# The activation of 32 clamped-SwiGLU experts: Silu on ScalarE, a clamp on the product, and three VectorE steps in place of five

## What is computed

```python
logits = xt @ w_router + b_router                # top 4 of 32, softmax over the four
gu = xblk @ w_gu[e] + b_gu[e]                    # 1024 -> 2048, gate half | linear half
x_glu = jnp.minimum(gu[:, :F], 7.0)
x_lin = jnp.clip(gu[:, F:], -7.0, 7.0)
act = x_glu * jax.nn.sigmoid(1.702 * x_glu) * (x_lin + 1.0)
return act @ w_down[e] + b_down[e]               # weighted by the gate and summed per token
```

## Time and profile before

| | us |
|---|---|
| median of 3 runs | 1244.47 |
| lowest, highest run | 1243.40, 1245.21 |
| span of the profiled execution | 1242.5 |

### The profile page before, as it was taken

The page is one execution under the profiler, slowest core; times in us unless marked ns, Lnnn a source line. Parts: engine busy times, 40 slices in busy tenths (PEclk is TensorE's granted clock), DMA queues, the critical chain, the costliest instruction groups (busy, mean ns, idle before and its releaser), DMA issues.

```text
span 1242.5 us, 40004 instructions
## 1 busy us (share of the span) xinstructions
PE 1147.6 (92%) x17556; PEld 886.8 (71%) x17557; DVE 1148.4 (92%) x870; ACT 933.7 (75%) x823; POOL 503.6 (41%) x69
## 2 busy tenths in 40 slices
PE   5999999999999999999999999999999999999984
PEld 3454556977777777777777777777777777888751
DVE  5855577989999999999999999999999999999987
ACT  4334444878888888888888888888888888888852
POOL 0110400027777776667766666631010011266620
PEclk9999999999999999999999999999999999999998
DMA  9605854999999999999999999999999999999986
GB/s 349 221 9 203 297 189 160 337 349 404 420 417 415 419 416 416 418 416 416 415 418 416 418 412 420 420 416 409 419 413 419 411 410 415 421 415 418 413 330 248
DMA packets 73255, 458.08 MB, mean 369 GB/s; under 512 B 10076, under 2 KB 10588, under 8 KB 23632
## 3 DMA queue, kind: packets, MB, share of 16 engines
q1 hardware_dynamic: 68480, 445.30, 88.5%
q0 software_dynamic: 3472, 8.21, 1.7%
q10 hardware_dynamic: 1152, 2.19, 0.6%
HBM read 443.26 MB, written 24.77 MB: 377 GB/s over the span
## 4 chain that ended last, share of the span: by engine, by line
PE 45%; DVE 32%; issue 19%; ACT 3%; DMA 1%; DVEq 0%; SPq 0%; ACTq 0%
DVE ring L416 22%; PE ps L437 16%; PE ps L473 11%; PE ps L1130 8%; PE ps L430 3%; PE ps L1233 3%; ACT ring L413 1%; DVE arena L503 1%; DVE arena L506 1%; DVE arena L518 1%; DVE arena L509 1%; DVE arena L512 1%; DMA ring<-in_w_in_dram 1%; PE ps L1170 1%; PE ps L458 1%
## 5 line engine op out<-in xcount | busy, mean ns | idle before, releaser
L495 POOL DMA_INDIRECT planes<-arena,slot_row x31 | 480.5, 15502 | 568.4 <-ACT arena L525 568.4
L416 DVE SCALAR_TENSOR_TENSOR ring<-ring 128x2048 f16<-128x2048 f32 x290 | 660.0, 2333 | 5.9 <-ACT ring L413 5.3
L413 ACT ACTIVATE ring<-ring 128x2048 f16<-128x2048 f32 x290 | 544.0, 1905 | 47.3 <-DMA ring<-in_w_gu_dram 25.4
L437 PE MATMUL ps<-arena,ring 128*128 128x88 f16 x12288 | 505.7, 205 | 44.4 <-issue 24.2
L437 PEld LDWEIGHTS ps<-arena,ring 128*128 128x128 f16 x12288 | 489.2, 100 | 54.5 <-issue 37.9
L473 PE MATMUL ps<-ring,arena 128*88 128x512 f16 x1536 | 338.9, 380 | 4.1 <-DVE arena L518 2.6
L473 PEld LDWEIGHTS ps<-ring,arena 128*88 128x88 f16 x1536 | 182.3, 121 | 147.1 <-issue 6.3
L416 DVE SCALAR_TENSOR_TENSOR ring<-arena,ring 128x2048 f16<-128x2048 f32 x94 | 215.7, 2334 | 1.2 <-ACT ring L413 1.1
L413 ACT ACTIVATE ring<-arena 128x2048 f16<-128x2048 f32 x94 | 178.3, 1905 | 9.1 <-DMA arena<-in_w_gu_dram 6.5
L430 PE MATMUL ps<-arena 128*128 128x88 f16 x2048 | 92.1, 205 | 8.3 <-issue 8.0
L430 PEld LDWEIGHTS ps<-arena 128*128 128x128 f16 x2048 | 84.5, 100 | 10.1 <-issue 10.0
(11 more groups left out here) (161 smaller groups left out, 600.9 us busy)
## 6 DMA issues: line engine op xcount, KB each, us to landing
ring<-in_w_gu_dram SPq DMA_DIRECT2D x194, 1024.0 KB, 12.1
ring<-in_w_down_dram SPq DMA_DIRECT2D x96, 1024.0 KB, 11.8
arena<-in_w_gu_dram SPq DMA_DIRECT2D x62, 1024.0 KB
arena<-in_w_down_dram SPq DMA_DIRECT2D x32, 1024.0 KB
ring<-in_w_in_dram SPq DMA_DIRECT2D x4, 2048.0 KB, 12.6
ring<-planes SPq DMA_DIRECT2D x6, 1024.0 KB, 10.0
ring<-in_w_out_dram SPq DMA_DIRECT2D x2, 2048.0 KB, 8.4
arena<-in_x_dram SPq DMA_DIRECT2D x4, 512.0 KB, 11.5
```

The source lines that it names most:

```text
L413: return act.activation(split_of(slot)[:, 0, :], raw(r), ACT.Copy, scale=SCALE_W)
L416: return dve.scalar_tensor_tensor(split_of(slot)[:, 1, :], raw(r), SCALE_W, split_of(slot)[:, 0, :], ALU.mult, ALU.subtract)
L437: mm = pe.matmul(o, w[:, i, cols], src[:, j, k, :], start=start and n == 0, stop=stop and n == 2, skip_group_check=True)
L495: return pool.indirect_dma_start(out=planes, out_offset=bass.IndirectOffsetOnAxis(ap=rows, axis=0), in_=y_row[0:SCAT, :], in_offset=None, ...
```

## The change

The sigmoid and the eviction of the gate half become one Silu on ScalarE straight from PSUM, of alpha * x. The upper clamp at 7 moves behind it: Silu rises wherever it is positive, so a minimum with Silu(alpha * 7) does the same, and it is folded into the product. The plus one of the linear half is added to the bias once, and the linear half is clipped to -6 and 8. The factor 1/alpha goes into the scale of the last steps. The tiles of the gate half now fill PSUM banks 0 and 1, those of the linear half banks 2 and 3. Five VectorE steps per expert become three; ScalarE has two as before, the first now reading PSUM.

The bias matmuls of the next expert wait for both engines (gu_taken and glu_ready). On ScalarE Silu stands ahead of conversion 1 of the next stage, where the sigmoid stood behind it; on VectorE the product stands behind conversion 1, where it stood behind conversion 0. For expert 0 Silu stands where ScalarE has just taken expert 1's columns and slots, ahead of conversion 5.

```diff
+SILU_MAX = ALPHA * LIMIT / (1.0 + math.exp(-ALPHA * LIMIT))
+ACT_SCALE = SCALE_A * UNSCALE / ALPHA
...
-        gub = reg_h[:, 2112:2112 + NF * CAP].rearrange("p (b h c) -> p b h c", b=GB, h=2)
-        sig = reg_d[:, 1024:1024 + KD * CAP].rearrange("p (b c) -> p b c", b=GB)
+        gub = reg_h[:, 2112:2112 + NF * CAP].rearrange("p (h b c) -> p h b c", h=2, b=2)
...
         def gu_cols(b, j):
-            return every_other(F * (j // 2) + 2 * b * P + j % 2)
+            f = PER * (b % 2) + j
+            return every_other(F * (b // 2) + 2 * (f // 2) * P + f % 2)
...
-        def dve_glu(dve):
-            return dve.tensor_scalar(gub[:, :, 0], GU[:, :, 0:2 * CAP], LIM, UNSCALE, ALU.min, ALU.mult)
+        def act_glu(act):
+            return act.activation(gub[:, 0], GU[:, 0:2, :], ACT.Silu, scale=ALPHA * UNSCALE)
 
         def dve_lin(dve):
-            return dve.tensor_scalar(gub[:, :, 1], GU[:, :, 2 * CAP:4 * CAP], LIM, -LIM, ALU.min, ALU.max)
+            return dve.tensor_scalar(gub[:, 1], GU[:, 2:4, :], (1.0 + LIMIT) / UNSCALE, (1.0 - LIMIT) / UNSCALE,
+                                     ALU.min, ALU.max)
 
         def dve_prod(dve):
-            return dve.scalar_tensor_tensor(gub[:, :, 1], gub[:, :, 1], 1.0 / UNSCALE, gub[:, :, 0], ALU.add, ALU.mult)
-
-        def dve_act32(dve):
-            return dve.scalar_tensor_tensor(gub[:, :, 1], gub[:, :, 1], SCALE_A * UNSCALE, sig, ALU.mult, ALU.mult)
+            return dve.scalar_tensor_tensor(gub[:, 1], gub[:, 0], SILU_MAX, gub[:, 1], ALU.min, ALU.mult)
 
         def act_ah(act):
-            return act.activation(actT[:, 0].rearrange("p (b j) c -> p b (j c)", b=GB), gub[:, :, 1], ACT.Copy)
+            return act.activation(act_parts(0), gub[:, 1], ACT.Copy, scale=ACT_SCALE)
 
         def dve_al(dve):
-            return dve.tensor_tensor(actT[:, 1].rearrange("p (b j) c -> p b (j c)", b=GB), gub[:, :, 1],
-                                     actT[:, 0].rearrange("p (b j) c -> p b (j c)", b=GB), ALU.subtract)
-
-        def act_sig(act):
-            return act.activation(sig, gub[:, :, 0], ACT.Sigmoid, scale=ALPHA)
+            return dve.scalar_tensor_tensor(act_parts(1), gub[:, 1], ACT_SCALE, act_parts(0), ALU.mult, ALU.subtract)
...
+            pool.wait_ge(bgu_loaded, 32)
+            pool.tensor_scalar(bgu_raw[:, F:2 * F], bgu_raw[:, F:2 * F], 1.0, None, ALU.add).then_inc(bgu_shifted, 1)
             pool.wait_ge(zeroed, 16 * TOP_K)
...
                     act.wait_ge(bgu_loaded, 32)
+                    act.wait_ge(bgu_shifted, 1)
...
-            def sigmoid(e):
-                act.wait_ge(glu_ready, e + 1)
-                act_sig(act).then_inc(sig_ready, 1)
+            def glu(e, done, first=False):
+                act.wait_ge(chunk_used, done)
+                if not first:
+                    act.wait_ge(prod_ready, e)
+                act_glu(act).then_inc(glu_ready, 1)
 
             def act_high_part(e):
-                act.wait_ge(act32_ready, e + 1)
+                act.wait_ge(prod_ready, e + 1)
...
                 if not last:
                     slots(s)
+                glu(s - 1, nth(s - 1, GU_CH))
                 high(h, q, 1)
-                sigmoid(s - 1)
                 high(h, q, 2)
...
             slots(1)
+            glu(0, GU_CH, first=True)
             high(0, 1, 5)
-            sigmoid(0)
...
                 pe.wait_ge(gu_taken, s)
+                pe.wait_ge(glu_ready, s)
                 pe_bias(pe, s)
...
                 low(h, q, 0)
+                low(h, q, 1)
                 multiplied(s - 1)
-                low(h, q, 1)
                 low(h, q, 2)
-                activated(s - 1)
                 low(h, q, 3)
```

More of the change, by code:

```diff
@@ L21 @@
+import math
 from contextlib import ExitStack
@@ L249, in build_program @@
         consts_made = sem("consts_made")
+        bgu_shifted = sem("bgu_shifted")
         bgu_high = sem("bgu_high")
@@ L304, in build_program @@
         low_ready = sem("low_ready")
-        act32_ready = sem("act32_ready")
         ah_ready = sem("ah_ready")
@@ L327, in build_program @@
         more = {k: sem(f"more_{k}") for k in ("high", "low", "used", "onehot", "gathered", "xT",
-                                              "glu", "lin", "prod", "sig", "act32", "ah", "act",
+                                              "glu", "lin", "prod", "ah", "act",
                                               "row", "stored", "meta_done", "meta", "pad")}
@@ L498, in pool_scatter, with act_parts @@
                                            bounds_check=ROWS_K - 1, oob_is_err=False)
-        LIM = LIMIT / UNSCALE
-        def dve_glu(dve):
-            return dve.tensor_scalar(gub[:, :, 0], GU[:, :, 0:2 * CAP], LIM, UNSCALE, ALU.min, ALU.mult)
+        def act_parts(i):
+            return actT[:, i].rearrange("p (b j) c -> p b (j c)", b=2)
+        def act_glu(act):
+            return act.activation(gub[:, 0], GU[:, 0:2, :], ACT.Silu, scale=ALPHA * UNSCALE)
         def dve_lin(dve):
-            return dve.tensor_scalar(gub[:, :, 1], GU[:, :, 2 * CAP:4 * CAP], LIM, -LIM, ALU.min, ALU.max)
+            return dve.tensor_scalar(gub[:, 1], GU[:, 2:4, :], (1.0 + LIMIT) / UNSCALE, (1.0 - LIMIT) / UNSCALE,
+                                     ALU.min, ALU.max)
         def dve_prod(dve):
-            return dve.scalar_tensor_tensor(gub[:, :, 1], gub[:, :, 1], 1.0 / UNSCALE, gub[:, :, 0], ALU.add, ALU.mult)
-        def dve_act32(dve):
-            return dve.scalar_tensor_tensor(gub[:, :, 1], gub[:, :, 1], SCALE_A * UNSCALE, sig, ALU.mult, ALU.mult)
+            return dve.scalar_tensor_tensor(gub[:, 1], gub[:, 0], SILU_MAX, gub[:, 1], ALU.min, ALU.mult)
         def act_ah(act):
-            return act.activation(actT[:, 0].rearrange("p (b j) c -> p b (j c)", b=GB), gub[:, :, 1], ACT.Copy)
+            return act.activation(act_parts(0), gub[:, 1], ACT.Copy, scale=ACT_SCALE)
         def dve_al(dve):
-            return dve.tensor_tensor(actT[:, 1].rearrange("p (b j) c -> p b (j c)", b=GB), gub[:, :, 1],
-                                     actT[:, 0].rearrange("p (b j) c -> p b (j c)", b=GB), ALU.subtract)
-        def act_sig(act):
-            return act.activation(sig, gub[:, :, 0], ACT.Sigmoid, scale=ALPHA)
+            return dve.scalar_tensor_tensor(act_parts(1), gub[:, 1], ACT_SCALE, act_parts(0), ALU.mult, ALU.subtract)
         def act_row(act, half, rows, scale):
@@ L1034, in _ @@
             stage(E // 2 - 1, 1, last=True)
-            sigmoid(E - 1)
+            glu(E - 1, nth(E - 1, GU_CH))
             high(E // 2, 0, 0)
@@ L1069, in one @@
                     more_high(c)
-                act.wait_ge(more["glu"], n)
-                act_sig(act).then_inc(more["sig"], 1)
-                act.wait_ge(more["act32"], n)
+                act.wait_ge(more["used"], CH * (n - 1) + GU_CH)
+                act_glu(act).then_inc(more["glu"], 1)
+                act.wait_ge(more["prod"], n)
                 act_ah(act).then_inc(more["ah"], 1)
@@ L1084, in skip @@
                 act.sem_inc(more["high"], CH)
-                for k in ("meta", "sig", "ah"):
+                for k in ("meta", "glu", "ah"):
                     act.sem_inc(more[k], 1)
@@ L1350, in _ @@
             pe.wait_ge(gu_taken, 1)
+            pe.wait_ge(glu_ready, 1)
             pe_bias(pe, 1)
@@ L1373, in _ @@
             pe.wait_ge(gu_taken, E)
+            pe.wait_ge(glu_ready, E)
             for t in range(NT):
@@ L1725, in taken @@
                     dve.wait_ge(act_ready, e)
-                dve_glu(dve).then_inc(glu_ready, 1)
                 dve_lin(dve).then_inc(gu_taken, 1)
@@ L1781, in _ @@
             low(0, 1, 4)
+            low(0, 1, 5)
             multiplied(0)
-            low(0, 1, 5)
-            activated(0)
             low(0, 1, 6)
@@ L1801, in _ @@
             multiplied(E - 1)
-            activated(E - 1)
             low(E // 2, 0, 0)
@@ L1815, in one @@
                 dve.wait_ge(more["used"], CH * (n - 1) + GU_CH)
-                dve_glu(dve).then_inc(more["glu"], 1)
                 dve_lin(dve).then_inc(more["lin"], 1)
@@ L1820, in one @@
                 dve_prod(dve).then_inc(more["prod"], 1)
-                dve.wait_ge(more["prod"], n)
-                dve.wait_ge(more["sig"], n)
-                dve_act32(dve).then_inc(more["act32"], 1)
                 dve.wait_ge(more["ah"], n)
@@ L1832, in skip @@
                 dve.sem_inc(more["low"], CH)
-                for k in ("onehot", "glu", "lin", "prod", "act32", "act"):
+                for k in ("onehot", "lin", "prod", "act"):
                     dve.sem_inc(more[k], 1)
```

5 lines of the change are left out of this document (removed).

## The result

The changed kernel takes 1245.77 us, the median of 17 runs (1243.74 to 1248.56), against 1243.40 us for the kernel before (17 runs taken with them, 1241.26 to 1245.91). The ratio is 1.0021, with a 95% interval of 1.0013 to 1.0029: **slower by 1.6 to 3.6 us**. The forecast was 1243.0 us, 1.5 us faster. One of the eight runs of the late-handover kernel further down took 1476.1 us at a granted clock of 0.751, and its figures there are those of the other seven.

What follows compares the result with a forecast made beforehand. VectorE was taken to pace single experts and the always-busy load queue the whole loop; 0 (middle) + 0.7 (start) - 2.2 (end) = -1.5 us from 1244.5 gave 1243.0 us, range 1235 to 1249.

Steps and rivals of the forecast that it cites:

- my case: The main forecast for the whole kernel: 1240.8 to 1246.5 us, chance 0.60.
- The middle: Expert loop: VectorE's 1.60 us saved per expert counts nothing, since the load queue needs 31.16 us per expert.
- Rival (a): Load queue in the loop has 1% more to give: -8 us, 1235 us; chance 0.15.
- rival (b): Expert loop: VectorE is the only bound, so the kernel takes 1197 us; chance 0.04.
- Rival (c): Expert loop: TensorE's issue waits become the bound, 31.45 us per expert, 1251 us; chance 0.16.
- Rival (d): ScalarE: Silu and Copy need different tables, two loads per expert, about 1244 us; chance 0.05.
- The start: First bank handover to expert 1: TensorE starts 1.8 us later, costing +0.2 to +1.8 us, taken as +0.7.
- The end: Last expert: VectorE converts the last awaited chunk 2.2 us earlier, so -2.2 us, bounds -0.8 and -2.9.
- The scatters: GpSimd's indirect DMA in each expert: all should become short, off the path, worth nothing.
- The bias: GpSimd's plus-one pass before the loop: at most 4.48 us, ended by 168 us, free.

Runs made afterwards that it cites:

- late-handover kernel: Kernel before, with TensorE's bias matmuls of expert 1 also waiting for ScalarE's Sigmoid of expert 0: 1249.51 us, ratio 1.0044.
- light kernels: Kernel before and changed kernel, each loading only half of every down-weight chunk: 1239.55 us and 1207.77 us.
- ballast: Changed kernel with two unused VectorE products per expert where the two removed steps stood: 1246.17 us, ratio 1.0024.
- light change: Changed kernel loading only the first half of each down-weight chunk: 1207.77 us, ratio 0.9704.
- early-table: Changed kernel with a one-column Silu ahead of the loop that brings in the table: 1242.72 us, ratio 0.9989.
- reordered kernels: Changed kernel with the table loaded ahead of the loop and expert 0's steps moved earlier: 0.9976, repeated 0.9966; with kept tokens also loaded sooner, 0.9975.
- light kernel before: Kernel before, loading only the first half of each down-weight chunk: 1239.55 us, ratio 0.9965.

## Why the prediction was wrong

The measured 1245.77 us lies inside the stated range, and inside that of my case. It lies on the other side of no change: the middle was right, and the two terms at the ends were both off, in the same direction.

**The middle: right.** VectorE's saving is hidden by the queue: 31.15 us for each of the late experts, as forecast (31.16), with VectorE at 29.4 to 29.9 busy. The light kernels show the cover directly: with it the saving is worth 1 to 2 us, without it 32. Rival (a) falls because the queue, full from the fourth expert on, still needs 31.15 us for one; rival (b) falls with the same rows. Rival (c) had the right sign for another reason: TensorE's issue waits at L438 went from 3.1 to 4.0 us in the four early experts and from 6.9 to 8.1 us in the four late ones, but the mean expert stayed at 31.15 us. (In rival (a), 1% of 895 us is 9 us, not 8.) Rival (d) falls: one table load in the loop.

**The start: the right place, mis-sized.** The step that failed is "Between +0.2 and +1.8 us; I take +0.7, nearer the low end since the lateness of VectorE shrinks before the queue is full". The lateness of the handover was near the forecast (2.0 us, 1.8 forecast). But it doesn't get smaller on its way into the loop. At 60 MB the queue is late by 1.6 to 2.0 us, and in the five-step kernels it stays so to the end (ballast, late handover). Measured over the pairs it costs 1.3 us per us: about +2.6 us where +0.7 was put, and outside the upper bound. The sum let TensorE work through at full pace behind the handover and had no term for its clock. The 4.26 us of standing were followed by 3.4 us at half clock in the change both times, in the ballast and in the light change, and 6.09 us by 6.8 us in the late handover; with 2.84 us or less at this place the clock stayed full in the seven others. The three-step kernels do make up 0.9 to 2.3 us between 60 and 150 MB, as argued. But part of it is given back later, and what is left is VectorE's saving, which the sum had already counted once, at the end.

**The end: -2.2 was too much, and not what happens there.** The step was that the last chunk is converted 2.2 us earlier because VectorE's lag is gone. The lag did go, but I held the landings of the earlier trace rows fixed. In the changed kernels the queue is the later of the two until the last weight, and it loses between 350 and 434 MB what it had gained: 1.3, 0.7, 1.1, 0.4, 0.3 and 1.0 us in the six three-step kernels, against 0.0, 0.6 and 0.1 in the five-step ones. Two sources are in the trace. The scatter ahead of the last one is short now. GpSimd's timeline of the kernel before and of the changed one:

```profile
1170.39 17.32 POOL L495 DMA_INDIRECT planes<-arena,slot_row  x1 [10.91 <-ACT arena L525]
```

```profile
1170.85 1.97 POOL L497 DMA_INDIRECT planes<-arena,slot_row  x1 [28.59 <-ACT arena L522]
```

Counted from the common moment its packets moved from 1033 to 1036 us before, up to 8 us after ScalarE took a chunk that it waited for at 1186.29 us (1028.4 by that count). In the change they move from 1020 to 1024, and ScalarE gets the same chunk at 1032.4, 3.9 us later. Between 1020 and 1030 the queue moved 4.19 MB of loads and no scatter before, and 3.88 MB of loads with 0.29 MB of scatter after. The last scatter then shares the engines with what the full queue still holds: 5.7 to 6.0 us instead of 4.3, though the other five-step kernels have 4.9 to 5.8 too. That these two make up the whole loss of the stream is argued from the traces; no kernel without one of them was run, and in the early-table and reordered kernels the scatter's packets are over before 1021 us, yet the stream loses 0.3 to 1.1 us. What remains of the end and the saving together is 1 to 2 us (1.4 by the lines), within the bounds of -0.8 and -2.9 but far from -2.2.

**The scatters: right in the trace** (all but the first two at 0.9 to 4.2 us, 18.57 in the earlier trace rows) and wrong in the price: "Only ScalarE waited for them, off the path: nothing" left out that a transfer that is issued sooner takes its place in a full queue sooner (argued, as under the end).

**The bias: right.** The pass takes 4.83 us ("at most" 4.48 was said) and ends at 161.1 us; ScalarE takes the biases from 182.1 on.

So the sum reads 0 + 2.6 - 1.4 = +1.2 us in place of 0 + 0.7 - 2.2 = -1.5 us; the two readings are +2.6 and +0.9. The 2.6 is about 0.9 x 2.0 for the lateness and the rest for the clock.

## What to carry to other kernels

Where a queue that is always full covers an engine's work, taking work off that engine gives next to nothing (here 1 to 2 us of 46), and the moment when the queue gets going at the start decides: look for the first handover of a shared buffer, and put nothing new into it, a table load least of all. Then look at TensorE's granted clock behind each place where it stands longer than before: a wait of 2 us more can cost nearly that much again in half-speed work. Moving the cheap step (here one index step of VectorE and one chunk of ScalarE) ahead of a bulk conversion at that place was worth as much (1.6 to 1.8 us) as the two steps taken off every one of 32 experts. Before counting a gain at the end of a stream, ask whether the last landing stays where it is.

## What the hardware showed beyond that

- GpSimd's indirect DMA takes 17 to 23 us while VectorE works without a gap on float32 operations with two inputs in SBUF, and 0.9 to 4.4 us in an expert that leaves VectorE gaps. In the light kernel before, where VectorE is busy for 30.87 of 30.87 us, the mean over 31 is 20964 ns; in the kernel before it is 15502 ns and in the changed one 3058 ns. The ballast alone brought the long ones back. ScalarE waited for it at times (60.4 us in all in the light kernel before), which moved no expert there.

```profile
L495 POOL DMA_INDIRECT planes<-arena,slot_row x31 | 649.9, 20964 | 395.9 <-ACT arena L525 395.9
```

- What ends a long one is not a gap. The twelve traces have 146 scatters of over 5 us, and all of them end 0.6 to 1.1 us after the start of VectorE's next eviction out of PSUM, the step with no input pair in SBUF. The one at 1170.39 us ends at 1187.71, and the eviction starts at 1186.81. So its length is the time to that step. By what mechanism was not tested.
- The clock fell behind every stop of 4.26 us or more ahead of the first handover (five kernels), and behind none of 2.84 us or less there (seven). A shorter stop can do it elsewhere: ahead of the last product of the loop TensorE stands for 2.56 us in every kernel, and a stretch of 3.4 us at half clock starts 2 to 4 us after the start of this stop in six of the twelve, the kernel before among them, and not in the changed one.
- The granted clock goes with the time from run to run. In the 68 runs of the kernel before that were taken with the experiments, the time falls by about 0.7 us for each 0.001 of clock (correlation -0.63). The mean clock is 0.9934 in the 17 runs of the change and 0.9938 in the 12 of its repetition, against 0.9946 in the 31 runs of the kernel before beside the latter and 0.9950 with the early table. A stretch of 3.4 us at half clock is 0.0014.
- A late start costs more than its own length (1.3 us per us). The clock accounts for it in size, not by a run of its own. The columns behind the handover of the change are 2.7 us late where the handover is 2.0 us late, though TensorE lost 1.7 us of work there: it waits for "issue" ahead of that gather for 0.45 us instead of 1.25.
